# RWKV scan: earlier store of the masked products, and half of the block loads issued by GpSimd

## The chip, the cores and the metric

One core of one Trainium2 chip runs the whole program. The metric is device time in microseconds. Before the change three runs gave 3704.3, 3705.8 and 3710.14 us; the median is 3705.8 us.

## What is computed

The reference is two transformer-like blocks over 1024 tokens of width 1024. The change touches one piece of the first block, the RWKV-7 recurrence, which runs once forwards and once backwards over the 1024 tokens for 8 heads of 64 channels:

```python
def step(S, inp):
    r_t, w_t, k_t, v_t, kk_t, b_t = inp
    sa = jnp.einsum('bhij,bhj->bhi', S, -kk_t)
    S = (S * w_t[:, :, None, :] + sa[..., None] * b_t[:, :, None, :]
         + v_t[..., None] * k_t[:, :, None, :])
    return S, jnp.einsum('bhij,bhj->bhi', S, r_t)
```

Everything around it (projections, the GLA scan, the feed-forward layers, attention) is the same in both kernels.

## The kernel before, in words

The recurrence is computed in chunks of 64 tokens, 16 of them (NSUB), each with both directions d = 0, 1 and 4 head pairs, so 8 lanes. Inside a chunk the step-by-step recurrence turns into matrices of 64 x 64: products of the scaled kk and b rows, masked to a strict triangle (tile NM), and the inverse of the identity plus that triangle. The inverse is made in two stages. First the four 16 x 16 blocks on the diagonal of each triangle are inverted by substitution on VectorE (`substitute_dve`, L1595 to L1616: a copy at L1601, 15 pairs of a multiply at L1614 and a subtract at L1615, a last copy at L1616). Then two levels of matmuls join the blocks to the full inverse.

The substitution wants a layout that the products do not have: all 64 blocks of a chunk side by side, on 32 partitions. So the data takes two trips through DRAM, all issued on SyncE's queue (SP) by `rwkv_scan_sp`:

- the trip there: SP waits for the masked products of chunk n (`dve["nm", n, 1]`), writes them to DRAM (L1431, 256 KB), waits for the landing, and loads the diagonal blocks into N16 with 16 loads of 4 KB (L1435: 8 blocks k, 2 directions d, rows of 64 bytes in DRAM);
- the trip back: SP waits for the substitution (`dve["x16", n]`), writes Z16 to DRAM (L1438, 128 KB), waits for the landing, and loads the inverted blocks onto the diagonal of ZZ with 8 loads of 16 KB (L1444, 64 bytes at a time).

In SP's program the trip there of chunk n + 1 stands behind the whole trip back of chunk n, and in front of it, for every even chunk, one load of 512 KB (`sig`, L1429) of the decay rows of the next pair of chunks.

The engines run a software pipeline. In one turn, with n the chunk whose products are made and m = n - 1, VectorE does in this order: the state add of chunk n - 2 (L1653); the masks NM and MM of chunk n (L1658); the output add (L1665); the scaled rows of chunk n + 1, `products(n + 1)` (L1639 to L1644); the state scale (L1670); the two joining levels for chunk m (L1674, L1678, L1682, L1685), which use ZZ of chunk m; and last the substitution of chunk n, which uses N16 of chunk n. TensorE's joining matmuls of chunk m wait for the ZZ loads (L1525), as

```python
pe.wait_ge(self.t_z["in", m])
```

and for every even chunk TensorE has 16 more matmuls in the turn, the running sums of the decays (`cum`, L1470). GpSimd has nothing in the scan but one memset at its start (L1592); its queue then stands until the next stage.

NM has three buffers, ZZ two, N16 and Z16 one each, and the two scratch areas in DRAM (`nd`, `zd`) two halves each.

Of the kernel before, what the change touches and what calls it, by code (L numbers as in the profile page):

```python
# [20 lines left out]
NBLK = TOK // PART  # L21
# [4 lines left out]
NSUB = 16  # L26
# [89 lines left out]
class Count:  # L116
# [4 lines left out]
    def __init__(self, nc, name, step):  # L121
        self.sem, self.step, self.n, self.at = nc.alloc_semaphore(name), step, 0, {}
# [89 lines left out]
class Kernel:  # L212
    def __init__(self, nc, ins, out):
        self.nc, self.i, self.out = nc, ins, out
        self.counters = []
        self.pe = self.engine("pe", nc.tensor)
        self.act = self.engine("act", nc.scalar)
        self.dve = self.engine("dve", nc.vector)
        self.pool = self.engine("pool", nc.gpsimd)
        self.sp = self.engine("sp", nc.sync)  # L220
        self.engines = (self.pe, self.act, self.dve, self.pool, self.sp)
        self.t_misc, self.t_h, self.t_st, self.t_in = (self.transfer(n) for n in ("t_misc", "t_h", "t_st", "t_in"))
        self.t_n, self.t_z, self.t_keep = (self.transfer(n) for n in ("t_n", "t_z", "t_keep"))
        self.t_k, self.t_r = ([self.transfer(f"{n}{k}") for k in range(8)] for n in ("t_k", "t_r"))
        self.t_b = [self.transfer(f"t_b{k}") for k in range(4)]
        self.t_lat = [self.transfer(f"t_lat{k}") for k in range(2)]
        self.t_x = [self.transfer(f"t_x{k}") for k in range(3)]
        self.t_a = [self.transfer(f"t_a{k}") for k in range(4)]
        self.t_w = [self.transfer(f"t_w{n}") for n in range(2)]
        self.t_d = [self.transfer(f"t_d{n}") for n in range(2)]  # L230
        self.t_out = [self.transfer(f"t_out{n}") for n in range(2)]
        self.ps = nc.alloc_psum_tensor("ps", [PART, 8, HALF], F32)
        self.room, self.made, self.also = 0, 0, {}
        self.dram = {}
        for n, shape in (("h", (NBLK, PART, D)), ("rows", (4, D)), ("la", (NBLK, PART, 512)), ("sg", (2, NBLK + 1, PART, RW)), ("lo", (3, PART, TOK)),
                         ("nd", (2, LANES, PART, CH)), ("zd", (2, 8, 4, 2, 2, 16, 16)), ("v", (PART, 4, TOK)), ("y_gla", (PART, 4, TOK)),
                         ("rpb", (HEADS, RPB_R, GRID, PART))):
            self.dram[n] = nc.dram_tensor(f"{n}_dram", shape, F32, kind="Internal").ap()
# [1180 lines left out]

    def rwkv_scan_sp(self):
        sp, sg, pe, dve = self.sp, self.dram["sg"], self.pe, self.dve
        nd, zd = self.dram["nd"], self.dram["zd"]
        for n in range(NSUB):
            if n % 2 == 0 and n // 2 + 1 < NBLK:
                t = n // 2 + 1
                sp.wait_ge(pe["cum", t - 1, 1])
                sp.e.dma_start(self.sig[:], sg[:, t].rearrange("d p c -> p d c")).then_inc(*self.t_in.one("sig", t))  # L1429
            sp.wait_ge(dve["nm", n, 1])  # L1430
            sp.e.dma_start(nd[n % 2].rearrange("l p c -> p l c"), self.NM[n % 3][:, :, 0, :]).then_inc(*self.t_n.one("out", n))  # L1431
            sp.wait_ge(self.t_n["out", n])
            for k in range(8):
                for d in range(2):
                    sp.e.dma_start(self.N16[4 * k:4 * k + 4, d], nd[n % 2, 4 * d:4 * d + 4, 16 * k:16 * k + 16, 16 * (k % 4):16 * (k % 4) + 16]) \  # L1435
                        .then_inc(*self.t_n.one("in", n))
            sp.wait_ge(dve["x16", n])
            sp.e.dma_start(zd[n % 2].rearrange("k x d w i c -> (k x) (d w i c)"), self.Z16[:].rearrange("p d w i c -> p (d w i c)")) \  # L1438
                .then_inc(*self.t_z.one("out", n))
            sp.wait_ge(self.t_z["out", n], self.pool["zero"])  # L1440
            if n >= 2:
                sp.wait_ge(pe["l4", n - 2, 1], dve["zz", n - 2, 1])
            for k in range(8):
                sp.e.dma_start(self.ZZ[n % 2][16 * k:16 * k + 16, :, :, :, 16 * (k % 4):16 * (k % 4) + 16].rearrange("i x d w c -> i (x d w) c"),  # L1444
                               zd[n % 2, k].rearrange("x d w i c -> i (x d w) c")).then_inc(*self.t_z.one("in", n))
        self.meet(sp, "rwkv_scan")

    def hb(self, d, b, at=0):
# [25 lines left out]
    def rwkv_scan_pe(self):  # L1474
        pe, act, dve, ps = self.pe, self.act, self.dve, self.ps
        for u in range(-2, NSUB):
            n, m = u + 2, u + 1
# [44 lines left out]
                    tr.then_inc(*pe.one("tr", n, d))  # L1522
            if 0 <= m < NSUB:
                NM_m, ZZ, ZZ2 = self.NM[m % 3], self.ZZ[m % 2], self.ZZ2
                pe.wait_ge(self.t_z["in", m])  # L1525
                for d in range(2):
                    if n < NSUB:
                        pe.wait_ge(act["BKT", n, d])
                    else:
                        pe.wait_ge(dve["xt", u, d])  # L1530
                    self.heads_pe(d, 0, CH, 0, ((lambda l, H: NM_m[H, l, 0, :], lambda l, H: ZZ[H, l % 4, l // 4, 0, :]),), "p4", m, d)
# [57 lines left out]
        self.meet(act, "rwkv_scan")  # L1589

    def rwkv_scan_pool(self):
        self.pool.e.memset(self.S[0][:], 0.0).then_inc(*self.pool.one("zero"))  # L1592
        self.meet(self.pool, "rwkv_scan")

    def substitute_dve(self, n):  # L1595

        dve = self.dve
        dve.wait_ge(self.t_n["in", n])
        if n:
            dve.wait_ge(self.t_z["out", n - 1])  # L1600
        dve.c.tensor_copy(self.Z16[:, :, 1], self.eye16[:]).then_inc(*dve.one())  # L1601
        N, Z = self.N16[:, 0], self.Z16[:, 0, 1]

        def both(x, second, first, rest):
            return bass.AP(tensor=x.tensor, offset=x.offset + first, ap=[x.ap[0], [second - first, 2]] + rest)

        for s in range(15):
            p, q, k = 15 - s, s, 15 - s
            zn, nn = 512, 256
            part = self.tmp16[:, 0:2 * k * (s + 1)].rearrange("p (d i c) -> p d i c", d=2, i=k)  # L1610
            rows = both(Z, zn + (q + 1) * 16, p, [[16, k], [1, s + 1]])
            pivot = both(Z, zn + q * 16, p * 16 + p, [[0, k], [1, s + 1]])
            col = both(N, nn + (q + 1) * 16 + q, p, [[16, k], [0, s + 1]])
            dve.c.tensor_tensor(part, col, pivot, ALU.mult).then_inc(*dve.one())  # L1614
            dve.c.tensor_tensor(rows, rows, part, ALU.subtract).then_inc(*dve.one())  # L1615
        dve.c.tensor_copy(self.Z16[:, :, 0], self.Z16[:, :, 1].rearrange("p d i c -> p d c i")).then_inc(*dve.one("x16", n))  # L1616
# [1478 lines left out]
```

## Time and profile before

| | |
|---|---|
| median of three runs | 3705.8 us (3704.3 to 3710.14) |
| the profiled execution, its own time | 3703.68 us |
| its span in the trace | 3702.3 us |
| mean granted TensorE clock | 0.937 |
| busy share of the span: TensorE, VectorE, ScalarE, GpSimd | 89%, 61%, 27%, 10% |
| the RWKV scan | from 712 to 1172 us of the span, 460 us |
| in that stretch: TensorE, VectorE, ScalarE, GpSimd busy | 366.7, 317.0, 65.7, 0.0 us |

The scan is an eighth of the span. The shares of the whole span say little about it: only the rows of this stretch do. A busy TensorE is not TensorE at its peak, and idle time counts only where it delays the chain that ends last.

### The profile page before, as it was taken

To read this page: it belongs to the slowest core of one execution; us is meant where nothing else is said; L and a number is where in the kernel's file an instruction comes from. 1 tells how busy PE (TensorE), PEld (TensorE's weight loads), DVE (VectorE), ACT (ScalarE), POOL (GpSimd) and SP (SyncE) were. 2 spreads that over 40 slices of the span, in tenths; PEclk is the share of its full clock that TensorE was granted. 3 is DMA by queue.
4 is the path that set the end of the run, shared out by engine and by line. 5 is a ranking of instruction groups with operands and counts; after the bars stand their busy time and mean duration, and the time that the engine had idled before them with its cause. 6 is when DMAs were issued, how large, how long until landed. Compare 5 with 4: busy or idle time off the path is not lost.

```text
span 3702.3 us, 56646 instructions
## 1 busy us (share of the span) xinstructions
PE 3305.3 (89%) x24667; PEld 2742.9 (74%) x24667; DVE 2275.5 (61%) x3148; ACT 997.1 (27%) x1468; POOL 368.5 (10%) x202
## 2 busy tenths in 40 slices
PE   6988799788886799999999887999888989999997
PEld 4777667677775478888888676876666768888885
DVE  5757656667775444444444566997555656666666
ACT  4544243211111231111111344113445222112112
POOL 2520033200000400000000121000001001111110
PEclk9978698889898799999999999999999989999999
DMA  4410054221113111111111212113001111111111
GB/s 136 125 40 13 15 184 128 69 37 28 35 32 111 57 34 46 52 52 44 42 52 52 80 40 69 46 46 88 1 1 58 35 33 53 46 46 50 53 46 63
DMA packets 261535, 207.19 MB, mean 56 GB/s; under 512 B 86968, under 2 KB 223943, under 8 KB 260775
## 3 DMA queue, kind: packets, MB, share of 16 engines
q1 hardware_dynamic: 247463, 178.40, 16.5%
q10 hardware_dynamic: 13824, 25.17, 2.2%
q8 instruction: 193, 3.16, 0.4%
q14 instruction: 55, 0.45, 0.0%
HBM read 172.06 MB, written 29.64 MB: 54 GB/s over the span
## 4 chain that ended last, share of the span: by engine, by line
PE 69%; DVE 17%; ACT 6%; POOL 2%; issue 2%; DMA 2%; SPq 2%; ACTq 0%; DVEq 0%; POOLq 0%
PE ps L2009 22%; PE ps L2024 16%; PE ps L1872 5%; PE ps L640 3%; PE ps L641 3%; PE ps L642 3%; PE ps L1461 2%; PE ps L2757 2%; DVE Yc L2634 2%; DVE s_Z L1615 2%; DVE s_tmp L1614 2%; PE ps L2733 2%; POOL a_x L2384 1%; SPq L1435 1%; PE ps L2743 1%
## 5 line engine op out<-in xcount | busy, mean ns | idle before, releaser
L3051 DVE TENSOR_TENSOR H<-H,ps 128x1024 f32<-128x1024 f32 x256 | 312.5, 1221 | 181.5 <-PE ps L2024 174.7
L2174 DVE TENSOR_TENSOR fsum<-fsum,ps 128x1024 f32<-128x1024 f32 x168 | 205.1, 1221 | 312.6 <-PE ps L2024 310.1
L2024 PE MATMUL ps<-dh,hh 128*128 128x512 f32 x864 | 340.3, 394 | 20.3 <-DVE hl L1989 14.3
L2024 PE MATMUL ps<-dl,hh 128*128 128x512 f32 x864 | 338.5, 392 | 0.0
L2024 PE MATMUL ps<-dh,hl 128*128 128x512 f32 x864 | 338.4, 392 | 0.0
L2009 PE MATMUL ps<-hn_h,uh 128*128 128x512 f32 x704 | 275.9, 392 | 7.6 <-DVE ul L1713 5.2
L2009 PE MATMUL ps<-hn_h,ul 128*128 128x512 f32 x704 | 275.6, 391 | 0.0
L2009 PE MATMUL ps<-hn_l,uh 128*128 128x512 f32 x704 | 275.6, 391 | 0.0
L2009 PE MATMUL ps<-hx_h,uh 128*128 128x512 f32 x512 | 201.4, 393 | 7.8 <-DVE hx_l L1989 5.3
L2024 PEld LDWEIGHTS ps<-dh,hh 128*128 128x128 f32 x864 | 163.8, 190 | 58.3 <-DVE hl L1989 16.0
L2009 PE MATMUL ps<-hx_l,uh 128*128 128x512 f32 x512 | 201.0, 393 | 0.0
L2009 PE MATMUL ps<-hx_h,ul 128*128 128x512 f32 x512 | 200.8, 392 | 0.0
L2024 PEld LDWEIGHTS ps<-dh,hl 128*128 128x128 f32 x864 | 163.5, 189 | 34.5
L2024 PEld LDWEIGHTS ps<-dl,hh 128*128 128x128 f32 x864 | 163.9, 190 | 33.6
L2384 POOL TENSOR_TENSOR a_x<-a_x,a_t 128x512 f32<-128x512 f32 x84 | 128.9, 1534 | 339.3 <-ACT a_t L2373 336.9
L2009 PEld LDWEIGHTS ps<-hn_h,uh 128*128 128x128 f32 x704 | 133.3, 189 | 36.0 <-DVE ul L1713 5.6
L2634 DVE SCALAR_TENSOR_TENSOR Yc<-cp,cols,Yc 128x1024 f32<-128x1024 f32 x120 | 154.2, 1285 | 4.3
L2009 PEld LDWEIGHTS ps<-hn_h,ul 128*128 128x128 f32 x704 | 133.2, 189 | 27.9
L2009 PEld LDWEIGHTS ps<-hn_l,uh 128*128 128x128 f32 x704 | 133.2, 189 | 27.7
L3021 POOL TENSOR_TENSOR dw<-dw,g_row 128x1024 f32<-128x1024 f32 x32 | 78.5, 2454 | 709.5 <-DMA dw<-in_w_mlp_dram 709.5
L640 PE MATMUL ps<-hx_h,cw 128*128 128x512 f32 x320 | 129.7, 405 | 18.1 <-DVE cw L620 8.4
L3030 ACT ACTIVATE relu<-ps 128x1024 f32<-128x1024 f32 x32 | 32.9, 1029 | 407.2 <-PE ps L2009 407.2
(472 smaller groups left out, 7682.4 us busy)
## 6 DMA issues: line engine op xcount, KB each, us to landing
aw<-in_w_ada_dram ACTq DMA_DIRECT2D x96, 256.0 KB, 3.0
uw<-in_w_mlp_dram SPq DMA_DIRECT2D x32, 512.0 KB, 4.3
dw<-in_w_mlp_dram SPq DMA_DIRECT2D x32, 512.0 KB, 5.1
uw<-in_ffn_gate_dram SPq DMA_DIRECT2D x22, 512.0 KB, 4.0
uw<-in_ffn_up_dram SPq DMA_DIRECT2D x22, 512.0 KB, 5.3
dw<-in_ffn_down_dram SPq DMA_DIRECT2D x22, 512.0 KB, 5.9
cw<-in_w_in_dram SPq DMA_DIRECT2D x20, 512.0 KB, 3.9
o_w<-in_w_out_dram SPq DMA_DIRECT2D x16, 512.0 KB, 13.1
```

What stands on the lines that cost most here:

```text
L640: pe.e.matmul(ps[0:m, 2 * (j % 2) + h, :], wh[:, k, :], xh, start=(k == 0), stop=False)
L641: pe.e.matmul(ps[0:m, 2 * (j % 2) + h, :], wh[:, k, :], xl, start=False, stop=False)
L642: mm = pe.e.matmul(ps[0:m, 2 * (j % 2) + h, :], wl[:, k, :], xh, start=False, stop=(k == kc - 1))
L1461: mm = pe.e.matmul(self.ps[H, 4 * d + b, at_x:at_x + r.shape[-1]], lhsT(4 * d + x, H), r, start=(n == 0), stop=(n == len(terms) - 1))
L1872: mm = pe.e.matmul(self.ps[:, 2 * (t % 2) + hf, :], x[a](k), w[b](k)[:, half(hf)], start=(n == 0 and m == 0), stop=(n == len(order) - 1 an ...
L2009: mm = pe.e.matmul(ps[:, 2 * pair + h, :], w[:, col], x[h][v][:, k, :], start=(k == 0 and m == 0), stop=(k == DC - 1 and m == 2))
L2024: mm = pe.e.matmul(ps[:, 2 * pair + hf, :], v[s][:, blk(t)], w[:, half(hf)], start=(m == 0), stop=(m == 2))
L2174: return dve.c.tensor_tensor(f, f, new, ALU.add) if g else dve.c.tensor_copy(f, new)
L2384: pool.c.tensor_tensor(acc[:], acc[:], self.a_t[who][:], ALU.add).then_inc(*pool.one("ada", q, who))
L2634: dve.c.scalar_tensor_tensor(out=o, in0=x[:, w:w + TOK], scalar=self.col("dw", n + 4 * w), in1=o, op0=ALU.mult, op1=ALU.add) \
L3021: pool.e.tensor_tensor(w, w, self.g2_row[:], ALU.mult).then_inc(*pool.one("m", "dw", g))
L3051: return dve.c.tensor_tensor(h, h, self.ps[:, 4 + 2 * (t % 2):6 + 2 * (t % 2), :], ALU.add)
```

## The change

`rwkv_scan_sp` gets another order, GpSimd issues half of the small loads, and two counters are added for them.

- SP, for chunk n: wait for the masked products of chunk n and write them to DRAM; then wait for chunk n - 1's Z16 in DRAM and load the even blocks k = 0, 2, 4, 6 of its inverse (4 loads); then wait for the products' landing and load the even blocks of N16 (8 loads); then, for odd n, the `sig` load; then wait for the substitution and write Z16. The first `sig` load stands ahead of the loop, the last 4 inverse loads behind it.
- GpSimd, for chunk n: wait for chunk n - 1's Z16 in DRAM and load the odd blocks of its inverse (4 loads); then wait for the products' landing and load the odd blocks of N16 (8 loads).
- TensorE and VectorE wait for both counters.

```diff
+        self.t_zb, self.t_nb = self.transfer("t_zb"), self.transfer("t_nb")
...
+    def blocks_there(self, eng, counter, n, ks):
+
+        nd = self.dram["nd"]
+        for k in ks:
+            for d in range(2):
+                eng.e.dma_start(self.N16[4 * k:4 * k + 4, d], nd[n % 2, 4 * d:4 * d + 4, 16 * k:16 * k + 16, 16 * (k % 4):16 * (k % 4) + 16]) \
+                    .then_inc(*counter.one("in", n))
+
+    def inverse_back(self, eng, counter, n, ks):
+
+        zd = self.dram["zd"]
+        if n >= 2:
+            eng.wait_ge(self.pe["l4", n - 2, 1], self.dve["zz", n - 2, 1])
+        for k in ks:
+            eng.e.dma_start(self.ZZ[n % 2][16 * k:16 * k + 16, :, :, :, 16 * (k % 4):16 * (k % 4) + 16].rearrange("i x d w c -> i (x d w) c"),
+                            zd[n % 2, k].rearrange("x d w i c -> i (x d w) c")).then_inc(*counter.one("in", n))
...
+        def sig(t):
+            sp.wait_ge(pe["cum", t - 1, 1])
+            sp.e.dma_start(self.sig[:], sg[:, t].rearrange("d p c -> p d c")).then_inc(*self.t_in.one("sig", t))
+
+        sig(1)
         for n in range(NSUB):
-            if n % 2 == 0 and n // 2 + 1 < NBLK:
-                t = n // 2 + 1
-                sp.wait_ge(pe["cum", t - 1, 1])
-                sp.e.dma_start(self.sig[:], sg[:, t].rearrange("d p c -> p d c")).then_inc(*self.t_in.one("sig", t))
             sp.wait_ge(dve["nm", n, 1])
             sp.e.dma_start(nd[n % 2].rearrange("l p c -> p l c"), self.NM[n % 3][:, :, 0, :]).then_inc(*self.t_n.one("out", n))
+            if n:
+                sp.wait_ge(self.t_z["out", n - 1], self.pool["zero"])
+                self.inverse_back(sp, self.t_z, n - 1, range(0, 8, 2))
             sp.wait_ge(self.t_n["out", n])
-            for k in range(8):
-                for d in range(2):
...
+            self.blocks_there(sp, self.t_n, n, range(0, 8, 2))
+            if n % 2 and (n + 3) // 2 < NBLK:
+                sig((n + 3) // 2)
             sp.wait_ge(dve["x16", n])
...
-            sp.wait_ge(self.t_z["out", n], self.pool["zero"])
-            if n >= 2:
-                sp.wait_ge(pe["l4", n - 2, 1], dve["zz", n - 2, 1])
-            for k in range(8):
...
+        sp.wait_ge(self.t_z["out", NSUB - 1])
+        self.inverse_back(sp, self.t_z, NSUB - 1, range(0, 8, 2))
         self.meet(sp, "rwkv_scan")
...
-                pe.wait_ge(self.t_z["in", m])
+                pe.wait_ge(self.t_z["in", m], self.t_zb["in", m])
...
     def rwkv_scan_pool(self):
-        self.pool.e.memset(self.S[0][:], 0.0).then_inc(*self.pool.one("zero"))
+        pool = self.pool
+        pool.e.memset(self.S[0][:], 0.0).then_inc(*pool.one("zero"))
+        for n in range(NSUB + 1):
+            if n:
+                pool.wait_ge(self.t_z["out", n - 1], pool["zero"])
+                self.inverse_back(pool, self.t_zb, n - 1, range(1, 8, 2))
+            if n < NSUB:
+                pool.wait_ge(self.t_n["out", n])
+                self.blocks_there(pool, self.t_nb, n, range(1, 8, 2))
...
-        dve.wait_ge(self.t_n["in", n])
+        dve.wait_ge(self.t_n["in", n], self.t_nb["in", n])
```

## Rows read from the trace of the kernel before

**Rows 1.** Stretches of one turn each: odd chunk 9, even chunk 10

```profile
core 0: us, PE busy (x) PEld busy (x) DVE busy (x) ACT busy (x) POOL busy (x), PEclk, DMA share, GB/s
958.10:983.70 25.60, 20.53 (x544) 19.66 (x544) 19.78 (x63) 2.73 (x6) 0.00 (x0) 0.93 0.17 26
983.70:1013.80 30.10, 25.66 (x560) 24.21 (x560) 19.90 (x64) 5.88 (x12) 0.00 (x0) 0.89 0.19 39
```

**Rows 2.** VectorE's waits in 712 to 1172: total, times, longest

```profile
DVE s_T L1682 <- PE ps L1461: 26.9, 16, 4.5
...
DVE s_Z L1601 <- DMA s_N<-nd_dram: 13.2, 8, 3.9
...
DVE s_T L1674 <- PE ps L1461: 5.3, 4, 1.7
```

**Rows 3.** TensorE's waits in 712 to 1172

```profile
PE ps L1461 <- DMA s_ZZ<-zd_dram: 24.3, 16, 3.0
```

**Rows 4.** SP's queue in odd chunk 9's turn: start, us

```profile
960.05 4.62 SPq L1444 DMA_DIRECT2D s_ZZ<-zd_dram  x8
964.72 0.45 SPq L1431 DMA_DIRECT2D nd_dram<-s_NM  x1
967.39 5.75 SPq L1435 DMA_DIRECT2D s_N<-nd_dram  x16
```

**Rows 5.** VectorE's instructions in the same turn: start, us

```profile
957.51 0.58 DVE L1616 COPY s_Z<-s_Z 32x512 f32<-32x512 f32 x1
...
958.68 1.27 DVE L1658 TENSOR_TENSOR s_NM<-ps,gram_mask 128x512 f32<-128x512 f32 x2
...
962.76 0.42 DVE L1640 TENSOR_TENSOR s_AR<-r_kk,s_Ex 128x256 f32<-128x256 f32 x1
...
964.25 0.17 DVE L1644 COPY s_last<-s_Ei 128x4 f32<-128x4 f32 x1
...
966.84 0.91 DVE L1674 TENSOR_TENSOR s_T<-ps,lev_mask 128x256 f32<-128x256 f32 x2
...
973.52 0.42 DVE L1685 TENSOR_TENSOR s_XT<-s_ZZ,ps 128x256 f32<-128x256 f32 x1 [0.32 <-PE ps L1461]
974.41 0.41 DVE L1601 COPY s_Z<-eye 32x512 f32<-32x512 f32 x1 [0.47 <-DMA s_N<-nd_dram]
```

**Rows 6.** The chain that ended last: a load's landing, and joining matmuls

```profile
972.81 1.58 DMA s_N<-nd_dram
...
1021.41 0.71 PE ps L1461 x16
```

**Rows 7.** Landing of the inverse loads, issue to landing

```profile
DMA to landing us min/median/max: 1.7/1.9/3.1
```

**Rows 8.** VectorE at the same places in even chunk 4

```profile
818.26 0.58 DVE L1616 COPY s_Z<-s_Z 32x512 f32<-32x512 f32 x1
...
829.03 0.74 DVE L1674 TENSOR_TENSOR s_T<-ps,lev_mask 128x256 f32<-128x256 f32 x2
...
838.17 0.41 DVE L1601 COPY s_Z<-eye 32x512 f32<-32x512 f32 x1
```

**Rows 9.** SP's queue in that even chunk

```profile
825.46 0.45 SPq L1429 DMA_DIRECT2D sig<-sg_dram  x1
...
830.58 5.76 SPq L1435 DMA_DIRECT2D s_N<-nd_dram  x16
```

**Rows 10.** Odd chunk 3: end and next start of the substitution

```profile
791.14 0.58 DVE L1616 COPY s_Z<-s_Z 32x512 f32<-32x512 f32 x1
...
809.51 0.41 DVE L1601 COPY s_Z<-eye 32x512 f32<-32x512 f32 x1
```

**Rows 11.** SP's queue, the first chunk's 16 loads

```profile
719.98 6.13 SPq L1435 DMA_DIRECT2D s_N<-nd_dram  x16
```

**Rows 12.** GpSimd's groups in the whole span: busy, mean ns

```profile
L2384 POOL TENSOR_TENSOR a_x<-a_x,a_t 128x512 f32<-128x512 f32 x84 | 128.9, 1534 | 339.3 <-ACT a_t L2373 336.9
...
L1417 POOL MEMSET s_ZZ<- 128x1024 f32 x2 | 1.8, 951 | 3.1 <-PE ps L642 3.1
```

More of the change, by code:

```diff
@@ L1424, in rwkv_scan_sp @@
         nd, zd = self.dram["nd"], self.dram["zd"]
+        def sig(t):
+            sp.wait_ge(pe["cum", t - 1, 1])
+            sp.e.dma_start(self.sig[:], sg[:, t].rearrange("d p c -> p d c")).then_inc(*self.t_in.one("sig", t))
+        sig(1)
         for n in range(NSUB):
-            if n % 2 == 0 and n // 2 + 1 < NBLK:
-                t = n // 2 + 1
-                sp.wait_ge(pe["cum", t - 1, 1])
-                sp.e.dma_start(self.sig[:], sg[:, t].rearrange("d p c -> p d c")).then_inc(*self.t_in.one("sig", t))
             sp.wait_ge(dve["nm", n, 1])
             sp.e.dma_start(nd[n % 2].rearrange("l p c -> p l c"), self.NM[n % 3][:, :, 0, :]).then_inc(*self.t_n.one("out", n))
+            if n:
+                sp.wait_ge(self.t_z["out", n - 1], self.pool["zero"])
+                self.inverse_back(sp, self.t_z, n - 1, range(0, 8, 2))
             sp.wait_ge(self.t_n["out", n])
-            for k in range(8):
-                for d in range(2):
-                    sp.e.dma_start(self.N16[4 * k:4 * k + 4, d], nd[n % 2, 4 * d:4 * d + 4, 16 * k:16 * k + 16, 16 * (k % 4):16 * (k % 4) + 16]) \
-                        .then_inc(*self.t_n.one("in", n))
+            self.blocks_there(sp, self.t_n, n, range(0, 8, 2))
+            if n % 2 and (n + 3) // 2 < NBLK:
+                sig((n + 3) // 2)
             sp.wait_ge(dve["x16", n])
@@ L1439, in rwkv_scan_sp @@
                 .then_inc(*self.t_z.one("out", n))
-            sp.wait_ge(self.t_z["out", n], self.pool["zero"])
-            if n >= 2:
-                sp.wait_ge(pe["l4", n - 2, 1], dve["zz", n - 2, 1])
-            for k in range(8):
-                sp.e.dma_start(self.ZZ[n % 2][16 * k:16 * k + 16, :, :, :, 16 * (k % 4):16 * (k % 4) + 16].rearrange("i x d w c -> i (x d w) c"),
-                               zd[n % 2, k].rearrange("x d w i c -> i (x d w) c")).then_inc(*self.t_z.one("in", n))
+        sp.wait_ge(self.t_z["out", NSUB - 1])
+        self.inverse_back(sp, self.t_z, NSUB - 1, range(0, 8, 2))
         self.meet(sp, "rwkv_scan")
```

## The prediction, made before the changed kernel ran

> **What bounds the kernel now.** I read the stretches of one turn each, then VectorE's and TensorE's waits in the scan, then the queue of SP and VectorE's instructions side by side. No engine is full in the scan: in a turn of 25.6 us VectorE is busy 19.8, and in one of 30.1 us 19.9 [rows 1]. The turn is a ring: masks of chunk n, joining of chunk n - 1, substitution of chunk n (8.75 us from its first copy to its last [rows 5]), and round again. Three strands run beside each other between one substitution's end and the next one's start, and the latest decides. I count from the end of the last copy, 958.09 in chunk 9 [rows 5].
>
> The *N strand*, the products' trip to DRAM: SP writes them only at 964.72, when the 8 inverse loads are issued, though VectorE had masked them at 959.95; they are there at 967.39, the 16 loads take 5.75, the last lands 1.58 after [rows 4 to 6]. N16 is ready at +16.3. The *ZZ strand*, the inverse's trip back: in DRAM at +1.96, 8 loads in 4.62, landing 1.9 [rows 4, 7], ready near +8.4, and a first half of the joining matmuls (0.7 [rows 6]) before VectorE can go on. VectorE's *own strand*: it is free for the joining only at 966.84, +8.75, and done with it at 973.94, +15.85 [rows 5]. So in chunk 9 all three end within half a microsecond, and shortening one alone brings nearly nothing.
>
> What the loads cost VectorE directly is 13.2 us in 8 waits for N16, the longest 3.9 (the first chunk's, which nothing precedes), so 9.3 over seven later chunks; waits for the joining's first matmuls are 5.3 us in 4 [rows 2]. TensorE's 24.3 us of waiting for ZZ [rows 3] is mostly behind VectorE's own strand. In even chunks the decay sums on TensorE stretch the turn (L1682 waits up to 4.5 [rows 2]): chunk 4's substitution starts at 838.17, +19.3, the earliest of its kind, and N16 is there just before it, at 837.9, though SP puts the 512 KB load first and the products land late behind it [rows 8, 9].
>
> **The change part by part.** *The earlier write.* The masks end at 959.95, +1.86 [rows 5]; write and landing take 2.67 (964.72 to 967.39 [rows 4]), so the products are in DRAM at +4.5 instead of +9.3. It holds the inverse loads up by nothing: Z16 is in DRAM at +1.96, and SP's write issues until +2.4; SP's own 4 inverse loads cost 4 x 0.58 and land near +6.6. SP's 8 loads of N16 run from +4.7 at 0.36 each (5.75 / 16 [rows 4]) and land by +9.2. SP is out of the way.
>
> *The decay load* moves behind SP's N16 loads, in odd chunks. It costs SP 0.45 [rows 9] before a wait for the substitution that ends later anyway; the sums that use it come a turn later. It shares the DMA engines with GpSimd's loads, but those are busy for only 17 to 19% [rows 1]. Nothing. If this cover is gone, GpSimd's last load lands later by up to its size, which no row prices alone; I leave it in the range.
>
> *GpSimd's half.* This decides. GpSimd issues 4 inverse loads from +1.96, and behind them 8 loads of N16: 12 issues in one queue, in order. Nothing else is queued there in the scan (0.00 busy [rows 1]), and nobody waits for it but TensorE's joining and VectorE's substitution, which are the two ends of the ring. The trace has no DMA issued by GpSimd. Bounds for one N16 load, u: from below SP's 0.36 per issue; from above 1.9, one load at a time from issue to landing [rows 7]. These lie far apart. The nearest rows on GpSimd itself are 0.95 for a memset that only writes SBUF and 1.53 for an elementwise instruction [rows 12]; the middle of the bounds, 1.1, lies between them, and I take u = 1.1. On SP an inverse load costs 0.58 to 0.36, 1.6 times as much, with four times the bytes; if what GpSimd adds is the same for every load, the ratio is smaller there, and I take 1.4 times, 1.54.
>
> N16's odd half is then there at 1.96 + 4 x 1.54 + 8 x 1.1 + 1.58 = +18.5, and ZZ's at 1.96 + 6.16 + 1.9 + 0.7 = +10.7 for VectorE. The products' earlier landing at +4.5 is hidden: GpSimd is not done with the inverse loads until +8.1.
>
> - Seven chunks like 9 (1, 5, 7, 9, 13, 15, and 14, which has no decay sums) start their substitution at +16.3 now and at +18.5 then: 7 x 2.2 = 15.4 us. ZZ's delay of 1.95 (10.7 for 8.75) lies inside this, since 15.85 + 1.95 = 17.8.
> - Two odd chunks with a slower TensorE, as chunk 3 (+17.8 [rows 10]) and 11: 2 x 0.7 = 1.4.
> - Six even chunks: N16 at +18.5 is before +19.3, hidden; but VectorE is free for the joining at +10.2 (829.03 less 818.84 [rows 8]) and ZZ comes at +10.7: 6 x 0.5 = 3.0.
> - The first chunk: 8 x 1.1 = 8.8 for 6.13 [rows 11], 2.7.
> - The last inverse: 6.16 for 4.62 [rows 4], 1.5.
>
> Sum +24.0 us, so 3703.7 + 24.0 = 3727.7 for an execution like the profiled one; its own time is 2.1 below the median of the runs, so **3730 us**.
>
> In general N16 is ready at 3.5 + 13.6 u, and the break-even with +16.3 is u = 0.94. The lower end of the bounds, u = 0.36, gives +8.4: no strand is late but VectorE's own, the 9.3 goes, most of the 5.3 goes, and some 2 us at both ends, -15 us. The upper end, 1.9, gives +29.3: 7 x 13.0 + 2 x 11.5 + 6 x 10.0 at most, and 9.1 and 6.0 at the ends, +190 us.
>
> The row for SP has 0.36 from issue to issue and 1.58 to the landing [rows 4, 6]. The Trainium skill, "DMA: Bandwidth & Descriptors", "Latency and other measured facts", gives about 1 us to the first byte for a DMA of GpSimd and about 0.6 for one of SP. If that were the whole difference, and both queues issued at one pace, the sum would be about -14 us in place of +24.0; no run here shows either figure.
>
> **The rivals.**
>
> *Faster: GpSimd issues nearly as fast as SP* (u up to 0.8, N16 by +14.4). For it: the loads are tiny, and the 16 issues of 0.36 are a third of the N strand, a share that two queues would halve. Against it: GpSimd's rows are 3 to 4 times SP's issue, and the gain has a ceiling, VectorE's own strand at +15.85. At u = 0.7: 9.3 and 0.5 at the first chunk, 3694 + 2 = 3696; at best 3691. TensorE's clock reads 0.93 and 0.89 of 2.4 GHz [rows 1]; less idle might keep it at the upper level for longer, which I leave unpriced.
>
> *No change within 0.2%* (about what a measurement of this kernel can tell from none, 7.4 us): u of 0.85 to 1.0, where N16 comes at +15.1 to +17.1. The early write gives about 5 us a chunk to the N strand and GpSimd's queue takes them back. 3706.
>
> *Much slower: GpSimd takes 1.4 us or more for a load, or is held up by VectorE.* From u = 1.25 on even the even chunks' cover (+19.3 and more) is broken and every chunk pays. At 1.4, N16 comes at +22.5: 7 x 6.2 + 2 x 4.7 + 6 x 3.2 + 8.3 at the ends, 80 us, 3786. For it: an inverse load is 256 pieces of 64 bytes, four times an N16 load's. A hold-up has its place in `products`, which runs while GpSimd issues: at least the two copies of 0.17, at most these and eight products of 0.42 [rows 5], so 0.3 to 3.7 us a chunk, +3 to +35 over the nine chunks that N16 bounds. The Trainium skill, "SBUF — State Buffer", "SBUF: two separate sides" and "Who interferes with whom", says that GpSimd cannot write its descriptors while VectorE runs a two-port copy in fp32, and that a two-input tensor_tensor does not stop it; by that rule only the two copies count, and no row here shows it.
>
> *The change does not do what it says*: SP's inverse loads now stand behind the masks' wait. Were the masks later than +1.96, the ZZ strand would pay. They end at +1.86 in chunk 9, and VectorE makes them straight after the last copy in every turn, so I give it nothing of its own.
>
> **How the numbers follow.** Slower by over 0.2% (u above 1.0): 0.57, of which 0.32 for the forecast (u of 1.0 to 1.25, 3714 to 3755) and 0.25 for the much slower one. Within 0.2%: 0.19. Faster by over 0.2%: 0.24. The range 3691 to 3790 reaches from the best case to u = 1.4 and leaves out 2 in 10, nearly all above.
>
> **What would show it.** Right: a GpSimd queue with 4 and 8 issues in a row, near 1.1 us apart; the products' write straight behind the masks; VectorE's L1601 waiting for N16 in nine or more chunks, 2 to 3 us more than now in each; the wait of TensorE for ZZ about 2 us longer a turn; the scan from 460 to about 485 us, nothing else moved. Wrong: L1601's waits gone and the odd turns below 25 us (issue under 0.8); or even turns growing as much as odd ones (issue above 1.25); or copies on VectorE that lengthen while GpSimd issues, which the sum does not have at all.

## The result, and the profile after

The changed kernel takes 3682.34 us, the median of five runs (3672.18 to 3689.17), against 3704.44 for five runs of the kernel before beside it (3695.29 to 3710.14): a ratio of 0.9941, with an interval of 0.9923 to 0.9959. It is faster by 0.6%, where 3730 us was forecast in a range of 3691 to 3790. The profiled execution took 3683.4 us, its span is 3682.1, its mean clock 0.941.

The queues first. Two stretches of the trace after: SP's and GpSimd's issues in odd chunk 9's turn (start, us, engine, line, operation), answering to [rows 4]:

```profile
946.96 0.32 SPq L1460 DMA_DIRECT2D zd_dram<-s_Z  x1
948.82 0.38 SPq L1451 DMA_DIRECT2D nd_dram<-s_NM  x1
949.29 2.15 SPq L1437 DMA_DIRECT2D s_ZZ<-zd_dram  x4
951.49 2.93 SPq L1428 DMA_DIRECT2D s_N<-nd_dram  x8
954.47 0.38 SPq L1446 DMA_DIRECT2D sig<-sg_dram  x1
```

```profile
949.16 2.24 POOL L1437 DMA_DIRECT2D s_ZZ<-zd_dram  x4 [18.61 <-DMA zd_dram<-s_Z]
951.72 4.92 POOL L1428 DMA_DIRECT2D s_N<-nd_dram  x8 [0.32 <-DMA nd_dram<-s_NM]
```

GpSimd's issues now have a price. The two load lines of the trace after (count, duration in ns as least/median/most, first and last start in us):

```profile
L1428 POOL DMA_DIRECT2D s_N<-nd_dram x128: 620/620/770, 724.1 to 1107.1; - x128
...
DMA to landing us min/median/max: 1.9/2.3/4.1
...
L1437 POOL DMA_DIRECT2D s_ZZ<-zd_dram x64: 562/568/575, 743.4 to 1124.2; - x64
...
DMA to landing us min/median/max: 1.9/2.9/4.2
```

An N16 load takes GpSimd 0.620 us and an inverse load 0.568, back to back: u is 0.62, not 1.1, and the load with four times the bytes is no dearer. Counted from the end of the last copy (946.93), GpSimd's last issue starts at +9.1 and ends at +9.7, and N16 is there at about +11.4 (2.3 for the landing, which the profile counts from the start of an issue).

VectorE in the same turn, from the end of one substitution to the start of the next, answering to [rows 5]:

```profile
946.35 0.58 DVE L1642 COPY s_Z<-s_Z 32x512 f32<-32x512 f32 x1
...
956.01 0.89 DVE L1700 TENSOR_TENSOR s_T<-ps,lev_mask 128x256 f32<-128x256 f32 x2 [0.28 <-PE ps L1479]
...
961.34 0.42 DVE L1711 TENSOR_TENSOR s_XT<-s_ZZ,ps 128x256 f32<-128x256 f32 x1 [0.32 <-PE ps L1479]
961.89 0.41 DVE L1627 COPY s_Z<-eye 32x512 f32<-32x512 f32 x1
```

The first copy waits for nothing any more and starts at +14.96, where it was at +16.32. The waits of VectorE and TensorE in the scan, 712 to 1141 us (total, times, longest), answering to [rows 2, 3]:

```profile
PE ps L1479 <- DMA s_ZZ<-zd_dram: 32.6, 16, 3.0
...
DVE s_T L1708 <- PE ps L1479: 25.9, 16, 3.6
DVE s_ZZ L1704 <- PE ps L1558: 19.4, 32, 1.3
DVE B L1691 <- PE ps L1479: 10.9, 18, 2.9
...
DVE s_T L1700 <- PE ps L1479: 5.3, 6, 3.2
...
DVE s_Z L1627 <- DMA s_N<-nd_dram: 4.5, 1, 4.5
```

The wait for N16 fell from 13.2 us in 8 to the first chunk's one of 4.5. TensorE waits 8.3 us longer for ZZ, and VectorE's wait behind it (L1700) is 5.3 as before, so that costs nothing. But two waits fell that no step of the prediction touches: those for the result of the first joining level (L1704) and for the outputs (L1691) were 30.1 and 25.0 before (L1678, L1665) and are 19.4 and 10.9. The stretches say why. After, the turns of chunks 5, 8, 9 and 14 and the whole ring, from the first substitution's end to the last one's (columns as in [rows 1]):

```profile
844.40:868.30 23.90, 19.15 (x544) 18.33 (x544) 19.79 (x63) 2.73 (x6) 7.17 (x12) 1.00 0.26 51
919.80:946.90 27.10, 22.67 (x560) 21.22 (x560) 19.80 (x64) 5.88 (x12) 7.17 (x12) 1.00 0.17 25
946.90:971.20 24.30, 19.15 (x544) 18.33 (x544) 19.91 (x64) 2.73 (x6) 7.16 (x12) 1.00 0.25 49
1073.30:1097.10 23.80, 19.15 (x544) 18.33 (x544) 19.68 (x63) 2.73 (x6) 7.17 (x12) 1.00 0.19 28
741.20:1120.20 379.00, 306.54 (x8096) 290.45 (x8096) 292.19 (x913) 59.81 (x126) 107.51 (x180) 0.98 0.20 35
```

The same view before, of even chunks 2 and 4, of chunks 5, 13 and 14 and of the ring:

```profile
761.60:791.70 30.10, 25.71 (x560) 24.22 (x560) 19.85 (x63) 5.88 (x12) 0.00 (x0) 0.89 0.20 40
818.80:847.50 28.70, 24.22 (x560) 22.77 (x560) 19.85 (x64) 5.88 (x12) 0.00 (x0) 0.94 0.21 41
847.50:873.60 26.10, 19.15 (x544) 18.33 (x544) 19.93 (x64) 2.73 (x6) 0.00 (x0) 1.00 0.17 26
1071.40:1097.00 25.60, 20.70 (x544) 19.88 (x544) 19.73 (x63) 2.73 (x6) 0.00 (x0) 0.93 0.17 26
1097.00:1122.80 25.80, 19.15 (x544) 18.33 (x544) 19.90 (x63) 2.73 (x6) 0.00 (x0) 1.00 0.17 26
736.70:1148.40 411.70, 330.79 (x8096) 314.13 (x8096) 292.41 (x914) 59.81 (x126) 0.00 (x0) 0.91 0.18 32
```

The same 8096 matmuls take 24.3 us less of TensorE, at a granted clock of 0.98 for 0.91, with VectorE's work unchanged. Three turns are at a clock of 1.00 (2.4 GHz) in both, with TensorE busy for 19.15 in both: chunks 5, 7 and 14 took 26.1, 25.7 and 25.8 us before, where VectorE waited 1.86, 1.84 and 1.98 for N16, and take 23.9, 23.9 and 23.8 now. That is the queues' part in such a turn, about 2 us. Before, an odd turn at 0.93 (25.6, chunk 13) was no longer than one at 1.00: N16 came at +16.3 to +16.7 either way, and what the clock gave VectorE's own strand was lost in the wait for it. Even turns have 30.1, 28.7 and 27.1 us at 0.89, 0.94 and 1.00, in order of the clock whatever the kernel.

The ring lost 32.7 us, and from its end to SP's first load for the next stage it is 20.9 us for 23.6 before, another 2.7. Of that the execution kept 20.2: the scan began 3.8 us later than before (same code in both), and behind it the clock stood at 0.68 to 0.71 of 2.4 GHz for 61 us where it had been 0.89 in the next stage's first 30. So two things have to be told apart: what the queues gave, and what the clock gave.

### The profile page after: what moved, and what is told of

The parts are those of the page before. It is cut to its first block, busy times and chain, and to the rows that moved or that the text cites. A ratio compares the mean times of both kernels' runs of the same rounds, so it can differ in the third digit from the quotient of the medians.

```text
span 3682.1 us, 56672 instructions
## 1 busy us (share of the span) xinstructions
PE 3289.4 (89%) x24667; PEld 2724.4 (74%) x24667; DVE 2275.2 (62%) x3148; ACT 997.1 (27%) x1468; POOL 484.3 (13%) x394
## 4 chain that ended last, share of the span: by engine, by line
PE 70%; DVE 17%; ACT 6%; POOL 3%; issue 2%; DMA 2%; SPq 1%; ACTq 0%; DVEq 0%; POOLq 0%
PE ps L2035 22%; PE ps L2050 16%; PE ps L1898 5%; PE ps L641 3%; PE ps L642 3%; PE ps L643 3%; PE ps L2783 2%; DVE Yc L2660 2%; PE ps L1479 2%; PE ps L2759 2%; DVE s_Z L1641 2%; DVE s_tmp L1640 2%; POOL a_x L2410 1%; PE ps L2769 1%; PE ps L1013 1%
## 5 line engine op out<-in xcount | busy, mean ns | idle before, releaser
L3047 POOL TENSOR_TENSOR dw<-dw,g_row 128x1024 f32<-128x1024 f32 x32 | 78.7, 2460 | 709.3 <-DMA dw<-in_w_mlp_dram 709.3
```

Source lines behind the costliest of these rows:

```text
L3047: pool.e.tensor_tensor(w, w, self.g2_row[:], ALU.mult).then_inc(*pool.one("m", "dw", g))
```

## The experiments

All are timed in rounds beside the kernel before. Because the clock turned out to matter, each is also read at equal clock. The 111 runs of the kernel before that stand beside them, on four chips, lie between 3682 and 3717 us, on a line over their mean granted clock (0.932 to 0.945): 3703.8 us at 0.937, and 2.8 us less for each 0.001 of clock, with 2.6 us of scatter about the line for 6.0 without it. "At equal clock" means the runs' mean distance from that line; it is a fit over executions, and no run sets the clock by itself.

**The order alone**, all 24 loads on SP (shortened, against the kernel before).

```diff
-            if n % 2 == 0 and n // 2 + 1 < NBLK: ... sig
             sp.wait_ge(dve["nm", n, 1]); write of the products
+            if n: inverse_back(sp, self.t_z, n - 1, range(8))
             sp.wait_ge(self.t_n["out", n])
+            self.blocks_there(sp, self.t_n, n, range(8)); sig for odd n
```

> The new order of SP's program alone; all 24 loads of a chunk on SP, GpSimd issues none. Clock theory (the gain is 9 us of VectorE's waits for N16 that go, and some 25 us because TensorE, whose gaps before the output matmuls no longer exceed 1.9 us, stays at 2.4 GHz): N16 is there at +1.9 (write) with 8 inverse loads to about +7, 16 loads to +12.8, landing +14.4, just in time, so the waits for N16 go, the clock of the scan rises from 0.90 to 0.93 or more, and the kernel gains 12 to 22 us. Issue theory (the gain comes from halving the issue time with the second queue): 0 to 8 us gained. Chance theory (TensorE's clock in the scan is luck of the run): clock anywhere, 9 us gained at most.

3704.93 us, ratio 0.9995 (0.9985 to 1.0005); at equal clock -0.2. VectorE's wait for N16 is gone but for the first chunk's 3.7, and TensorE and VectorE wait for the inverse instead. Two waits of the trace, then SP's queue in chunk 9's turn:

```profile
PE ps L1479 <- DMA s_ZZ<-zd_dram: 41.3, 16, 4.0
...
DVE s_T L1693 <- PE ps L1479: 15.3, 13, 3.9
```

```profile
955.82 4.93 SPq L1437 DMA_DIRECT2D s_ZZ<-zd_dram  x8
960.80 5.85 SPq L1428 DMA_DIRECT2D s_N<-nd_dram  x16
```

The write stands ahead of 8 inverse loads here, and the joining (L1693) waits 15.3 for the 5.3 of [rows 2]. The early write moves the wait from one strand to the other; alone it gives nothing in the time.

**The split alone**, in the old order (shortened; the lines of GpSimd as comments).

```diff
             self.blocks_there(sp, self.t_n, n, range(0, 8, 2))   # GpSimd: range(1, 8, 2)
             sp.wait_ge(dve["x16", n]); write of Z16
             self.inverse_back(sp, self.t_z, n, range(0, 8, 2))   # GpSimd: range(1, 8, 2)
```

> The old order (products written behind the inverse loads, the decay load first in even chunks), with the odd blocks issued by GpSimd at 0.62 and 0.56 us each. N16's halves land near +7.0 + 4.9 + 1.6 = +13.5 in odd chunks; in even chunks as late as before less 1 us. Clock theory: the waits for N16 go here too, clock 0.93 or more, 12 to 22 us gained, like the order alone; the two parts of the change are each enough. Issue theory: nearly the whole 22 us gained here, and little by the order alone. Chance theory: 9 us at most.

3695.68 us, 0.9976 (0.9963 to 0.9989); at equal clock -7.8. The wait for N16 is 5.1 us in 2. The second queue does most of it (7.8 of the change's 10.8 at equal clock, below): it shortens both trips at once.

**All 24 loads on GpSimd**, in the new order; SP's lines for them are left out.

```diff
-                self.inverse_back(pool, self.t_zb, n - 1, range(1, 8, 2))
+                self.inverse_back(pool, self.t_zb, n - 1, range(8))
-                self.blocks_there(pool, self.t_nb, n, range(1, 8, 2))
+                self.blocks_there(pool, self.t_nb, n, range(8))
```

> The new order, but all 24 loads on GpSimd. N16 at 1.96 + 8 x 0.56 + 16 x 0.62 + 2.0 = +18.4, which is what the prediction put for the change. If the prediction's sum was right but for the price of a load: seven chunks 2 us later, the others covered, 15 to 25 us slower than before. Clock theory: the waits for N16 of 2 us or more in most chunks open gaps on TensorE before the output matmuls, the clock of the scan is 0.90 or below, and it is 20 to 40 us slower than before.

3727.52 us, 1.0053 (1.0034 to 1.0073). GpSimd's queue in chunk 9's turn, and two of VectorE's waits:

```profile
971.86 4.47 POOL L1437 DMA_DIRECT2D s_ZZ<-zd_dram  x8 [15.62 <-DMA zd_dram<-s_Z]
976.32 9.84 POOL L1428 DMA_DIRECT2D s_N<-nd_dram  x16
```

```profile
DVE s_T L1698 <- PE ps L1477: 22.4, 16, 4.3
...
DVE s_Z L1625 <- DMA s_N<-nd_dram: 11.8, 6, 8.3
```

This puts N16 close to where the prediction had put it for the change: the last issue starts 15.9 us after the substitution (its end was 969.64), the landing comes at about +18, and the odd chunks' substitutions start at +18.0 to +19.0. The ring and the first chunk's wait grow by 15.3 and 4.4 us, and the time by 22.5, where the prediction's sum for +18.5 was 24.0. But it is not N16 alone that is late. Behind the first chunk VectorE waits for it only 3.5 us in 5 (chunk 9 does not wait for it at all), while its wait for the joining's first matmuls is 22.4 for the 5.3 before: the inverse comes late by about as much. The clock is lower too (0.933 in the mean), and at equal clock it is +9.2. So the agreement is of the whole and not of each term.

**Three quarters, and one quarter, of the loads on GpSimd.**

```diff
-                self.inverse_back(pool, self.t_zb, n - 1, range(1, 8, 2))
+                self.inverse_back(pool, self.t_zb, n - 1, (1, 2, 3, 5, 6, 7))
...
-                self.blocks_there(pool, self.t_nb, n, range(1, 8, 2))
+                self.blocks_there(pool, self.t_nb, n, (1, 2, 3, 5, 6, 7))
```

SP issues the other blocks, (0, 4). For one quarter GpSimd has (3, 7) and SP (0, 1, 2, 4, 5, 6).

> The changed kernel with GpSimd issuing 6 of the 8 inverse loads and 12 of the 16 N16 loads (half as the change, all as the run that was 22 us slower than before). N16 at 1.96 + 6 x 0.57 + 12 x 0.62 + 2.0 = +14.8, ZZ's last load 1.1 us later than in the change. Clock theory with feedback: VectorE's own strand at 2.4 GHz ends at +14.5, so only 0.3 us a turn is late directly (5 us in all), but turns of 25 us or more lose TensorE's upper clock: scan clock 0.90 to 0.93, 10 to 20 us slower than the change. Sum of delays alone: 5 us slower than the change, clock near 0.98.

> The changed kernel with GpSimd issuing a quarter only (2 inverse loads and 4 of N16), SP the rest. SP's inverse loads end near +5.9 plus 1.9, a microsecond later than in the change, N16 near +10.5 plus 1.6. Both strands are ready before VectorE is (+8.75, +14.5). Strand theory: within 5 us of the change. If the late inverse loads were what the order alone died of (TensorE waits 41 us for ZZ there, 33 in the change), a part of that comes back: 4 to 10 us slower than the change.

3691.89 us, 0.9968 (0.9954 to 0.9981), and 3685.61 us, 0.9954 (0.9934 to 0.9973); at equal clock -7.6 and -10.0. With three quarters N16 is waited for again (11.8 us in 5); with one quarter the time is the half's, within what can be told. The expectation that turns of 25 us or more lose the upper clock did not hold: with three quarters on GpSimd, the turns of chunks 4 and 10 took 27.1 us at 1.00.

**ScalarE's queue in GpSimd's place.**

```diff
+                act.wait_ge(self.t_z["out", u + 1], self.pool["zero"])
+                self.inverse_back(act, self.t_zb, u + 1, range(1, 8, 2))
...
+                act.wait_ge(self.t_n["out", u + 2])
+                self.blocks_there(act, self.t_nb, u + 2, range(1, 8, 2))
```

> The changed kernel with ScalarE's queue in GpSimd's place for the odd blocks: 4 inverse loads before its copies of BKT, 8 N16 loads behind them. If what counts is that two queues issue at once, whichever they are: within 5 us of the change (ScalarE has 70 us of work in 460). If GpSimd's price of 0.62 against SP's 0.36 still matters: up to 5 us faster than the change. Rival: the waits that ScalarE's queue now holds delay its copies (BKT, 1.2 us a turn) and TensorE behind them, 5 to 20 us slower than the change.

3691.98 us, 0.9973 (0.9958 to 0.9989); at equal clock -12.0. ScalarE's queue does it as well as GpSimd's. In the plain mean it is 9.7 us faster than the kernel before where the change is 15.8, since its runs had a clock of 0.9361 in the mean.

**A warmer TensorE**: six extra matmuls of 128x128x256 a turn, whose result nobody reads, in the kernel before and in the changed one.

```diff
             self.heads_pe(d, 3, CH, 0, ..., "ss", u, d)
+                for x in range(6 if d else 0):
+                    pe.e.matmul(ps[:, 2, 0:256], self.tri[:, 0, 0:PART], self.tri[:, 0, :], start=True, stop=True)
```

> The kernel before with 6 extra 128x128x256 fp32 matmuls per turn on TensorE, on a part of PSUM that is free, where it otherwise waits for the state (some 1.4 us at 2.4 GHz). Nothing of the loads is changed. Clock theory: clock of the scan 0.96 or more in place of 0.90, VectorE's waits for TensorE (L1665, L1678) fall by some 20 us in sum while its waits for N16 stay at 13 us or grow to 20, since a faster turn exposes them; 8 to 20 us gained. If the clock is set by something else, or does not matter: 0 to 8 us slower.

> The changed kernel with the same 6 extra matmuls a turn as in the run on the kernel before. Clock theory: the change already holds the scan at 0.98, so nothing is left to gain, within 5 us of the change, slower if the extra matmuls (1.4 us in a gap of 1.8) push the output matmuls. If the extra matmuls' 8 us on the kernel before came from anything else than the clock, they come here too.

3696.72 us, 0.9979 (0.9965 to 0.9993), and 3690.09 us, 0.9962 (0.995 to 0.9975). The runs' mean clock is 0.942 in both, where the kernel before has 0.937: added work raised the granted clock, and in the kernel before it paid for itself although its matmuls cost something (+8.3 at equal clock). In the changed kernel it did not; the ring was 398.3 us at a clock of 0.96. The extra matmuls stand ahead of the output matmuls, and VectorE waits for those 22.8 us, at most 4.1 at a time, for 10.9 and 2.9 in the change.

**The change again**, three times with twelve runs each, nothing edited.

> The changed kernel once more, unaltered. Over the runs so far, the kernel before takes 3.0 us less for every 0.001 of mean granted clock (58 runs, 0.932 to 0.940), and the five runs of the change lie at 0.942, which is 14 of their 22 us. If the change causes that clock: median within 5 us of 3682, mean clock 0.941 or more. If those five runs had luck, as ScalarE's half (clock 0.936, 12.5 us gained) suggests: mean clock 0.937 to 0.939, 3688 to 3694.

> The changed kernel, unaltered, a third time. If the change lets TensorE stay at 2.4 GHz in some executions (it did in 8 of 17 runs at a mean clock of 0.941 or more, against 2 of 87 of the kernel before): 2 to 7 of 10 to 12 runs at 0.941 or more, near 3672 to 3683 us, the rest at 3690 to 3701, and at most 1 in 10 of the kernel before. If the clock is luck of the chip and the hour alone: the same share in both kernels. In either case the run of the change lies 8 to 12 us below the line of the kernel before at the same clock.

> As the third: the same kernel under another name in the same call, for the count of runs. Its share of runs at 0.941 or more should be that of the third within what 12 runs can tell.

3697.22 us, 0.9968 (0.9944 to 0.9992); 3688.22, 0.9962 (0.9941 to 0.9983); 3689.11, 0.9954 (0.9936 to 0.9972). The last one's profiled execution is the same kernel at another clock; chunks 8 and 9 and the ring, and behind them chunk 13 and the ring of the first of the three:

```profile
924.20:954.40 30.20, 25.74 (x560) 24.24 (x560) 19.93 (x64) 5.89 (x12) 7.19 (x12) 0.89 0.15 23
954.40:981.00 26.60, 22.12 (x544) 21.32 (x544) 19.81 (x64) 2.74 (x6) 7.19 (x12) 0.87 0.23 45
732.70:1141.40 408.70, 339.61 (x8096) 323.19 (x8096) 292.44 (x914) 60.01 (x126) 107.83 (x180) 0.89 0.19 32
```

```profile
1068.80:1094.30 25.50, 20.70 (x544) 19.88 (x544) 19.75 (x63) 2.73 (x6) 7.19 (x12) 0.93 0.17 26
...
741.30:1141.90 400.60, 327.63 (x8096) 311.21 (x8096) 292.50 (x914) 59.88 (x126) 107.84 (x180) 0.93 0.19 33
```

Turn by turn this is the price of the clock: an even turn takes 27.1 us at 1.00 (2.4 GHz all through) and 30.2 at 0.89, chunk 9's 24.3 at 1.00 and 26.6 at 0.87. And in this slower execution VectorE's waits for the first level's result and the outputs are 34.5 and 24.6 us, no less than the 30.1 and 25.0 of the kernel before: that they fell in the first one was the clock.

```profile
DVE s_ZZ L1704 <- PE ps L1558: 34.5, 32, 1.8
...
DVE B L1691 <- PE ps L1479: 24.6, 21, 2.9
```
 Four profiled executions of the changed kernel have rings of 379.0, 382.5, 400.6 and 408.7 us at 0.98, 0.97, 0.93 and 0.89. At the 0.91 of the ring before, the last two give some 405 by the straight line between them, for 411.7. TensorE's busy time for the same 8096 matmuls tells the clock more finely (330.79 before, 327.63 and 339.61 in those two), and by it the line gives 402.7. So the part that the queues gave inside the ring is 7 to 9 us, and most of the 32.7 seen first was the clock. Where it lies can be read turn by turn: an even turn takes 30.2 at 0.89 with either kernel, an odd one at 0.93 takes 25.5 for 25.6, and one at 1.00 takes 23.9 for 25.7 to 26.1.

The rest of what the queues gave lies behind the ring. From the last substitution's end to SP's first load for the next stage it is 23.6 us before and 23.9 with the order alone, and 20.6 with the split alone and 20.6 to 20.9 in the four executions of the change, whatever the clock of their rings (22.5 with ScalarE's queue). The prediction had 1.5 us more here for the last inverse, and it is 2.7 to 3.0 less. SP's load, before and in the last execution of the change:

```profile
1172.06 0.36 SPq L1695 DMA_DIRECT2D r_hones<-in_k_head_ones_dram  x1
```

```profile
1162.35 0.36 SPq L1721 DMA_DIRECT2D r_hones<-in_k_head_ones_dram  x1
```

The last substitution ended at 1148.4 and 1141.5.

Over all 41 runs of the change the mean is 3687.4 us and the mean clock 0.9390, for 3703.2 and 0.9372 over the 111 before: 15.8 us less, of which 10.8 at equal clock.

**The decay sums earlier**: TensorE's sums stand ahead of its wait for ZZ instead of between the joining levels.

```diff
+            if u % 2 == 0 and (u + 4) // 2 < NBLK:
+                ...
+                self.cum_pe((u + 4) // 2)
             if 0 <= m < NSUB:
                 ...
-            if u % 2 == 0 and (u + 4) // 2 < NBLK:
-                ...
-                self.cum_pe((u + 4) // 2)
```

This was tried on the changed kernel, on the kernel before, on the variant with ScalarE's queue and on the one with a quarter.

> The changed kernel with TensorE's 16 decay-sum matmuls of the even turns moved ahead of the wait for ZZ, where TensorE stood 1.7 to 3 us a turn, away from between the two joining levels, where VectorE waited 3.6 us for them. Strand theory (VectorE's own strand and the joining matmuls bound the turns now, not the loads): even turns go from 27.1 to about 24.5 us, L1708's waits of 25.9 us fall to some 8, 7 x 2.6 = 18 us faster than the change, ratio to before about 0.989. Rival (the loads bound the turn): the joining starts no earlier and its start is pushed by the sums, 0 to 5 us.

> The early decay sums alone on the kernel before. Its inverse loads land near +8.4 and the sums then fill TensorE's wait of 1.0 to 1.4 us in even turns, but in the kernel before the decay load goes out only at +6.1 to +6.6 in the even turn itself and lands 4.2 later, so the sums start at +10.5 at the earliest and the joining matmuls stand behind them: VectorE waits some 3 us longer for the first joining and 3.6 less for the second. Strand theory: within 8 us of the kernel before, where the same edit gives 12 or more on the changed one, whose decay load goes a turn earlier.

> ScalarE's half in GpSimd's place, together with the early decay sums. If the two are independent: 12 us (ScalarE's half) or 22 (the change) plus some 15 of the early sums, so 3670 to 3680. If the loads must be early for the sums to pay, as the sums now stand in TensorE's wait for them: nearer 3685.

> A quarter of the loads on GpSimd and the early decay sums. Both alone: 10 us at equal clock for the quarter, as for the change's half; 31 us for half and early sums. Strand theory: ZZ's last load is the one that the sums need not wait for, so the same 28 to 32 us at equal clock, 3668 to 3676 in the median. Rival (SP's 6 inverse loads are late enough to matter once the sums no longer hide them): 20 to 26 us at equal clock.

On the changed kernel: 3669.98 us, 0.9911 (0.9892 to 0.9929), the fastest of all and 0.9% below the kernel before. With ScalarE's queue 3673.61, 0.9924 (0.9902 to 0.9947); with the quarter 3674.07, 0.9917 (0.9897 to 0.9936). At equal clock they are -31.5, -29.7 and -27.1, so 17 to 21 us more than the same kernels without the early sums. On the kernel before it is slower: 3718.2, 1.0044 (1.0029 to 1.0059), by more than the 8 us that were expected at most. Of the changed kernel with early sums one wait and the turn of chunk 8, and of the kernel before with them one wait and SP's load of the decays:

```profile
DVE s_T L1708 <- PE ps L1479: 7.2, 17, 0.5
```

```profile
901.10:926.00 24.90, 22.73 (x560) 21.28 (x560) 19.87 (x64) 5.88 (x12) 7.16 (x12) 1.00 0.18 28
```

```profile
PE ps L1470 <- DMA sig<-sg_dram: 23.2, 6, 5.4
```

```profile
995.13 0.45 SPq L1429 DMA_DIRECT2D sig<-sg_dram  x1
```

In the changed kernel, the wait of 25.9 for the second level's mask is 7.2, and an even turn at a clock of 1.00 takes 24.9 for 27.1. In the kernel before, TensorE stands 23.2 us for decays that SP loads only behind the inverse. So the change's quiet third part, the decay load in the turn before, looks like what lets the sums move; no run moved that load by itself.

## Why the prediction was wrong

The step that failed is "*GpSimd's half*", and in it "I take u = 1.1", with "1.54" for an inverse load. Measured are 0.62 and 0.568. The bounds, 0.36 and 1.9, held the truth; the value between them was chosen by rows of GpSimd's memset and elementwise work [rows 12], 0.95 and 1.53, which said nothing of the 0.62 that an issue takes there, and the ratio of 1.4 was carried over from SP, where the issue varies (a median of 0.323 and 0.469 for the two kinds in the trace after); on GpSimd it does not. Both errors point the same way. With the measured prices the prediction's own line gives N16 at 1.96 + 4 x 0.57 + 8 x 0.62 + 2.3 = +11.5, where the trace has about +11.4, far ahead of VectorE's own strand.

A smaller slip in the same line points the same way. The landing of 1.58 starts at 972.81 [rows 6], where the last of the 16 issues starts and not where it ends. Added behind the last issue, it makes N16 one issue too late: +17.4 would have followed from u = 1.1. The measured landing of 2.3 for 1.58 takes most of that back at the measured prices.

Point by point:

- *The three strands*: right. The order alone changes which one is late and not the time; in the change the waits for N16 went and VectorE's own strand was next. With all loads on GpSimd the whole costs about what the sum said, though most of it came with the inverse and the clock, where the sum had N16.
- *The rival "GpSimd issues nearly as fast as SP"*, with 0.24, is what happened, and its size of about -10 us for the queues is what the 41 runs show at equal clock (-10.8). It had 9.3 from the later chunks, which all went, and 0.5 at the first, where the wait rose from 3.9 to 4.5 instead: the second queue's landing and slower issue took it back.
- *Its end of 3691 as "at best"* was wrong. It rested on VectorE's own strand ending at +15.85, as if that were fixed. The strand contains joining matmuls; at a clock of 1.00 it ended at +14.8 in chunk 9. This is the second step that failed: the clock was named and left "unpriced", so its term stood at nothing. The trace before had the means to price it: even turns of 30.1 and 28.7 us at 0.89 and 0.94, with the same work, and odd turns at 1.00 in which VectorE had ended its strand by +14.9 and waited 1.8 to 2.0 for N16.
- *The hold-up by VectorE's two-port copies*: not seen. The copies at L1670 take 0.17 as before, one of them 0.20, and GpSimd's issues vary by little (562 to 575 ns for the inverse loads). Its price of "+3 to +35" was also slightly off, as 9 x 3.7 is 33. The Trainium skill, "SBUF — State Buffer", "Who interferes with whom", would have GpSimd's descriptors wait for such copies; with copies as short as these no wait of a size that matters shows.
- *The decay load costs nothing*: nothing in the traces speaks against it, and no run tests it by itself.
- *The pages' figures*: an inverse load that GpSimd issues lands 2.3 us after its issue where GpSimd has all of them, for 1.9 to 2.0 where SP has all of them. The Trainium skill, "DMA: Bandwidth & Descriptors", "Latency and other measured facts", gives 0.4 us more for GpSimd's first byte; the traces agree, with 0.3 to 0.4. The sum by that page, -14 us, was nearer to the result than mine, but it also took both queues to issue at one pace, and they do not.

What stays open is the clock's own share. The first five runs had a mean clock of 0.9418, and 13 of their 22 us were that; for some 8 of these they were a lucky five, since all 41 runs have 0.9390. Without that luck the forecast was still wrong, as the mean of 3687.4 lies below 3691 too. Of the change's 41 runs 15 had a clock of 0.941 or more, of the 111 runs before 3. That is more often than chance gives, and worth some 5 us in the mean. But the theory of the expectations, that shorter gaps between TensorE's bursts keep the clock up, did not hold as it was put: the order alone, the split alone and ScalarE's queue shorten or move the same gaps and had 0 of 11, 0 of 12 and 0 of 12, while three quarters and one quarter on GpSimd had 3 of 10 and 6 of 12. These counts are small, and no run tells what makes an execution fall into the upper group.

## What to carry to other kernels

Price an issue on the queue that will carry it, by one look at any kernel that issues from that engine; other work of that engine says nothing about it. Where two trips share one queue, swapping their order can merely move the wait, and a second queue shortens both. Where several strands end together, look for the one whose time does not follow the clock: it hides what a faster engine would give. Where runs of one kernel differ by more than the effect that is looked for, set each run beside its granted clock before believing a median of five.

## What was not expected of the hardware

- GpSimd issues a DMA in 0.56 to 0.62 us whether it moves 4 or 16 KB in pieces of 64 bytes, with little scatter (0.77 at most).
- The inverse loads' landing rose from 1.9 us [rows 7] to 3.0 on SP and 2.9 on GpSimd when the 256 KB write of the products was put just ahead of them and both queues issued at once. With both queues in the old order it was 2.0 and 2.2, and with the new order on SP alone 2.0; so it is the two together. With ScalarE as the second queue in the new order it was 2.7 on both.
- Executions of one kernel on one chip differ by up to 30 us with their mean clock, and the difference arises all over the program: code that both kernels share ended its last step ahead of the scan at 709.3 and at 713.1 us, and in the execution with early sums at 694.6.
- Six extra matmuls a turn, read by nobody, made the kernel before faster by 0.2%.
